# Down projection of a transformer layer as seven half-size products instead of eight

## The reference, cut to what matters

```python
def conv_ffn(h, w_up, conv_w, conv_b, w_down):
    z = h @ w_up                                  # 512 x 1024 times 1024 x 5632
    ...
    a, u = jnp.split(zc, 2, axis=-1)              # zc: a causal convolution of width 3 over z
    return (jax.nn.silu(a) * u) @ w_down          # 512 x 2816 times 2816 x 1024

x = x + conv_ffn(rms_norm(x, norm_ffn_g[l]), ...)
return rms_norm(x, final_norm_g)
```

## Time and profile before

| | us |
|---|---|
| median of 3 runs (965.14 to 965.41) | 965.34 |
| span of the profiled execution | 963.6 |
| around the span (median less span) | 1.7 |
| TensorE busy | 951.7 (99%) |
| VectorE busy | 563.3 (58%) |
| ScalarE busy | 390.9 (41%) |
| GpSimd busy | 34.6 (4%) |

### The profile page before, as it was taken

The page is one execution under the profiler, slowest core; times in us unless marked ns, Lnnn a source line. Parts: engine busy times, 40 slices in busy tenths (PEclk is TensorE's granted clock), DMA queues, the critical chain, the costliest instruction groups (busy, mean ns, idle before and its releaser), DMA issues.

```text
span 963.6 us, 12000 instructions
## 1 busy us (share of the span) xinstructions
PE 951.7 (99%) x4782; PEld 796.8 (83%) x4782; DVE 563.3 (58%) x646; ACT 390.9 (41%) x427; POOL 34.6 (4%) x27
## 2 busy tenths in 40 slices
PE   8999999999999999999999999999999999999997
PEld 6899889777888788888888878888888888888886
DVE  5877654554677564466545548776777677711123
ACT  6473223332664552333333446444434444311122
POOL 1000000200000000000021005000000000000000
PEclk9999999999999999999999999999999999999999
DMA  7414212122232523333223224343333432222212
GB/s 253 160 44 131 73 59 88 46 79 62 66 95 81 178 76 97 98 98 120 90 91 126 79 75 131 88 127 92 87 87 104 113 87 87 92 103 111 88 44 88
DMA packets 121570, 93.80 MB, mean 97 GB/s; under 512 B 3930, under 2 KB 115902, under 8 KB 121406
## 3 DMA queue, kind: packets, MB, share of 16 engines
q1 hardware_dynamic: 121534, 93.27, 31.4%
HBM read 91.16 MB, written 2.10 MB: 97 GB/s over the span
## 4 chain that ended last, share of the span: by engine, by line
PE 91%; DVE 4%; ACT 3%; issue 1%; DMA 0%; SPq 0%; DVEq 0%; ACTq 0%
PE ps L496 66%; PE ps L999 12%; PE ps L860 5%; DVE wL L1345 1%; PE ps L540 1%; PE ps L640 1%; PE ps L631 1%; PE ps L624 1%; ACT wH L1029 1%; PE ps L874 1%; PE ps L890 1%; ACT L1029 1%; PE ps L646 1%; DVE hgF L1345 0%; DVE hgG L1537 0%
## 5 line engine op out<-in xcount | busy, mean ns | idle before, releaser
L496 PE MATMUL ps<-hH,wH 128*128 128x512 f32 x784 | 308.5, 394 | 4.1 <-DVE wL L1345 3.8
L496 PE MATMUL ps<-hH,wL 128*128 128x512 f32 x784 | 305.3, 389 | 0.0
L496 PE MATMUL ps<-hL,wH 128*128 128x512 f32 x784 | 305.2, 389 | 0.0
L1345 DVE TENSOR_TENSOR wL<-raw,wH 128x2048 fp32r<-128x2048 f32 (+3 forms) x90 | 188.4, 2094 | 130.9 <-ACT wH L1029 130.7
L1029 ACT ACTIVATE wH<-raw 128x2048 fp32r<-128x2048 f32 (+3 forms) x90 | 157.7, 1752 | 227.5 <-PE ps L496 146.3
L496 PEld LDWEIGHTS ps<-hH,wH 128*128 128x128 f32 x784 | 147.2, 188 | 37.9 <-DVE wL L1345 5.6
L496 PEld LDWEIGHTS ps<-hH,wL 128*128 128x128 f32 x784 | 147.1, 188 | 31.0
L496 PEld LDWEIGHTS ps<-hL,wH 128*128 128x128 f32 x784 | 147.2, 188 | 30.0 <-issue 0.2
L999 PE MATMUL ps<-wH,actH 128*128 128x512 f32 x176 | 68.7, 390 | 0.0
L999 PE MATMUL ps<-wH,actL 128*128 128x512 f32 x176 | 68.5, 389 | 0.0
L999 PE MATMUL ps<-wL,actH 128*128 128x512 f32 x176 | 68.5, 389 | 0.0
(11 more groups left out here) (275 smaller groups left out, 1225.4 us busy)
## 6 DMA issues: line engine op xcount, KB each, us to landing
raw<-in_w_in SPq DMA_DIRECT2D x57, 512.0 KB, 4.1
raw<-in_w_up SPq DMA_DIRECT2D x44, 512.0 KB, 4.6
raw<-in_w_down SPq DMA_DIRECT2D x22, 512.0 KB, 3.9
raw<-in_w_branch SPq DMA_DIRECT2D x24, 256.0 KB, 4.3
raw<-in_w_out SPq DMA_DIRECT2D x8, 512.0 KB, 4.1
raw<-in_w_mkv SPq DMA_DIRECT2D x8, 512.0 KB, 4.4
xtok<-in_x SPq DMA_DIRECT2D x8, 256.0 KB, 4.4
xtok<-in_x SPq DMA_DIRECT2D x1, 2048.0 KB, 9.1
```

The lines of the kernel that those rows point to most:

```text
L496: last = pe.matmul(out_ap, a, b, start=start and k + m == 0, stop=stop and m == 2 and k == len(terms) - 1)
L1345: q.sig(dve.tensor_tensor(out_ap, a, b, op), sem)
```

## The change

The down projection is done by one level of Strassen's scheme (Winograd's form). Tokens, the 2816 channels and the 1024 output columns are each cut in two halves, and instead of eight products of halves there are seven, of sums of halves. The 1408 channels of a half make 11 pairs of 128-row blocks, and `NP` is 11.

The up projection takes its slots in another order, tile i of the first half and then tile i of the second, and `prod` goes into one array `pair` of seven half-token blocks of 256 for each pair, which VectorE completes with four additions (`act_sums`). `actH`, `actL`, ScalarE's copy and VectorE's subtraction of the activation go from the up loop. All 22 slots are still there, the last two written out after a loop of ten turns.

The down projection has 22 steps. In each of the first 11 ("upper") four products are done, 24 matmuls: ScalarE makes four upper parts (512, 1024, 512 and 1024 numbers wide), VectorE four lower parts of the same sizes and, in between, three sums of 512 from the raw weights of the next step (`weight_sums`). In each of the other 11 ("lower") three products are done, 18 matmuls: ScalarE copies 768, 1024 and 512, VectorE adds 512 and subtracts 768, 1024 and 512. Raw weights are loaded twice in part: 768 KB an upper step, 512 KB a lower one. Operands of a step are in two buffers by turns, and ScalarE's first copy into one waits for TensorE's end of the step two before (`d_done`). Between the upper and the lower steps VectorE combines the four finished products with additions of 1024 out of the banks, the residual's 32 transposes go into banks in groups of eight, and the lower steps add on top. The last two lower steps are done together, product by product and token tile by token tile, so that pieces finish one by one. ScalarE loads the table for the square roots in the fifth lower step. At the end VectorE adds the stored parts, ScalarE squares out of `otok`, GpSimd multiplies three pieces by the gain ahead of time, VectorE and ScalarE scale, and six DMAs store the output. The final gain's load goes behind the first two down loads in SyncE's order.

```diff
-        actH = at("actH", A, [P, KF, S], F32R)
-        actL = at("actL", A + 44 * KIB, [P, KF, S], F32R)
...
+        pair = at("pair", A, [P, NP, 7, HT])
...
-            def load_down(n, j):
-
-                v = raw[n.s][:, :].rearrange("p (k c) -> p k c", k=2)
-                load(n, *((v[:, k, :], wdn[:, 2 * j + k, :]) for k in range(2)))
+            def load_down(i):
+                n = Slot(N_DN + i)
+                if i < 2:
+                    sp.wait_ge(lo_ready, n.n(-1))
+                else:
+                    sp.wait_ge(d_lo, lows(i - 2, 1))
+                    sp.wait_ge(d_t, 2 * (i - 2) + 2)
+                rows = slice(P * i, P * i + P)
+                low = slice(FF // 2 + P * i, FF // 2 + P * i + P)
+                sp.dma_start(raw[n.s][:, 0:D], w_down[0, rows, :]).then_inc(raw_in[n.s], 16)
+                sp.dma_start(raw[n.s][:, D:D + S], w_down[0, low, S:D]).then_inc(raw_in[n.s], 16)
+            def load_lower(i):
+                g = NP + i
+                s = (N_DN + g) % 2
+                if i < 2:
+                    sp.wait_ge(d_lo, lows(g - 2, 1))
+                    sp.wait_ge(d_t, 2 * (g - 2) + 2)
+                else:
+                    sp.wait_ge(d_lo, lows(g - 2, 2))
+                    sp.wait_ge(d_t4, i - 1)
+                sp.dma_start(raw[s][:, 0:D], w_down[0, FF // 2 + P * i:FF // 2 + P * i + P, :]).then_inc(d_in[s], 16)
...
-            sp.wait_ge(slot_done, N_MO)
+            with sp.Fori(0, NP) as i:
+                for k in range(2):
+                    load_up(Slot(N_UP + k, i, 2), i + NP * k)
+            for i in range(2):
+                load_down(i)
+            sp.wait_ge(slot_done, N_DN)
             sp.dma_start(gainF[:, :], final_norm_g.partition_broadcast(P)).then_inc(g_row, 16)
-            with sp.Fori(0, KF // 2) as i:
...
+            lo_half, hi_half = slice(0, S), slice(S, D)
+            sp.wait_ge(o_fin, 1)
+            sp.dma_start(osrc[:, 2, :], otok[:, 2, :]).then_inc(out_done, 16)
+            sp.wait_ge(o_act, 1)
+            sp.wait_ge(o_fin, 2)
+            sp.dma_start(osrc[:, 3, :], otok[:, 3, :]).then_inc(out_done, 16)
+            sp.wait_ge(o_fin, 3)
+            sp.dma_start(osrc[:, 0, hi_half], otok[:, 0, hi_half]).then_inc(out_done, 16)
+            sp.wait_ge(o_act, 2)
+            sp.dma_start(osrc[:, 0, lo_half], otok[:, 0, lo_half]).then_inc(out_done, 16)
+            sp.wait_ge(o_fin, 4)
+            sp.dma_start(osrc[:, 1, hi_half], otok[:, 1, hi_half]).then_inc(out_done, 16)
+            sp.wait_ge(o_act, 3)
+            sp.dma_start(osrc[:, 1, lo_half], otok[:, 1, lo_half]).then_inc(out_done, 16)
+            sp.wait_ge(out_done, 16 * 6)
...
+            pool.wait_ge(g_row, 16)
+            pool.wait_ge(d_out, 5)
+            pool.wait_ge(d_lo, lows(NP, 0))
+            pool.tensor_tensor(g22[:, :], otok[:, 3, S:D], gainF[:, S:D], ALU.mult).then_inc(d_gain, 1)
+            for t in range(2):
+                pool.wait_ge(d_out, 6 + t)
+                pool.tensor_tensor(g11[:, t, :], otok[:, t, 0:S], gainF[:, 0:S], ALU.mult).then_inc(d_gain, 1)
...
+            def half_product(g, q, b, start, stop, tiles=(0, 1)):
+                s = (N_DN + g) % 2
+                for t in tiles:
+                    ah, al = (x[s][:, q, P * t:P * t + P] for x in (sH, sL))
+                    for m, (x, w) in enumerate(((ah, wH), (ah, wL), (al, wH))):
+                        last = pe.matmul(ps[:, b + t, :], x, w[s][:, S * q:S * q + S], start=start and m == 0,
+                                         stop=stop and m == 2, skip_group_check=True)
+                return last
...
+            for i in range(NP):
+                for q, b in enumerate((4, 6, 2, 0)):
+                    if q == 0:
+                        pe.wait_ge(d_lo, lows(i, 2))
+                    elif q < 3:
+                        pe.wait_ge(d_lo, lows(i, 2 + q))
+                    if i == 0 and q >= 2:
+                        pe.wait_ge(taken, N_DN - 3 + q)
+                    last = half_product(i, q, b, i == 0, i == NP - 1)
+                    if i == NP - 1:
+                        last.then_inc(d_sum, 1)
+                if i < NP - 1:
+                    last.then_inc(d_done, 1)
+            for i in range(NP - 2):
+                g = NP + i
+                for q, b in enumerate((4, 6, 0)):
+                    if i == 0:
+                        if q == 0:
+                            pe.wait_ge(d_m1, 1)
+                        else:
+                            pe.wait_ge(d_out, (1, 3)[q - 1])
+                        residual((2, 3) if q == 2 else (0, 1), range(4, 8) if q == 1 else range(4), b)
+                    pe.wait_ge(d_lo, lows(g, (2, 2, 3)[q]))
+                    last = half_product(g, q, b, False, False)
+                last.then_inc(d_done, 1)
+                if i == 0:
+                    pe.wait_ge(d_out, 4)
+                    residual((2, 3), range(4, 8), 2).then_inc(d_sum, 1)
+            for q, b in ((0, 4), (2, 0), (1, 6)):
+                for t in range(2):
+                    for g in (2 * NP - 2, 2 * NP - 1):
+                        pe.wait_ge(d_lo, lows(g, 3))
+                        last = half_product(g, q, b, False, g == 2 * NP - 1, (t,))
+                    last.then_inc(d_sum, 1)
...
-                hi(n + 2)
-                act.wait_ge(f_prod, n.n(1 - N_UP))
-                do(actH[:, bass.ds(n.n(-N_UP), 1), :], prod[:, :], ACT.Copy, f_hi)
...
+            def down_upper(i):
+                n = Slot(N_DN + i)
+                act.wait_ge(raw_in[n.s], n.loads())
+                if i < 2:
+                    act.wait_ge(slot_done, n.n(-1))
+                else:
+                    act.wait_ge(d_done, i - 1)
+                upper(i, wH[n.s][:, 0:S], raw[n.s][:, 0:S])
+                act.wait_ge(f_sum, 4 * i + 4)
+                upper(i, sH[n.s][:, :, :], pair[:, i, 0:4, :])
+                act.wait_ge(d_t, 2 * i + 2)
+                upper(i, wH[n.s][:, S:2 * S], t2_of(i))
+                upper(i, wH[n.s][:, 2 * S:4 * S], tsum[n.s][:, :, :].rearrange("p q c -> p (q c)"))
+            def lower_upper(i):
+                g = NP + i
+                s = (N_DN + g) % 2
+                if i == 1:
+                    act.wait_ge(d_sum, 4)
+                else:
+                    act.wait_ge(d_done, g - 1 if i == 0 else g - 2)
+                upper(g, sH[s][:, 0:3, :], pair[:, i, 4:7, :])
+                act.wait_ge(d_in[s], 16 * (i // 2 + 1))
+                upper(g, wH[s][:, 0:D], raw[s][:, 0:D])
+                act.wait_ge(d_t4, i + 1)
+                upper(g, wH[s][:, D:D + S], t2_of(i))
...
+            for i in range(NP):
+                lower_upper(i)
+                if i == 0:
+                    act.wait_ge(d_sum, 1)
+                    do(m1[:, :, :], ps[:, 4:6, :], ACT.Copy, d_m1)
+                if i == 4:
+                    act.wait_ge(d_out, 5)
+                    for t in (2, 3):
+                        square_of(t, 1, o_sum)
+                    do(ostat[:, 0, 5:6], eps[:, 0:1], ACT.Sqrt)
...
+            def act_sums(i):
+                j = bass.ds(i, 1)
+                dve.wait_ge(f_prod, i * 2 + 2)
+                tt(pair[:, j, 2, :], pair[:, j, 6, :], pair[:, j, 3, :], ALU.subtract, f_sum)
+                dve.wait_ge(f_sum, i * 4 + 1)
+                tt(pair[:, j, 1, :], pair[:, j, 0, :], pair[:, j, 2, :], ALU.add, f_sum)
+                tt(pair[:, j, 3, :], pair[:, j, 0, :], pair[:, j, 3, :], ALU.subtract, f_sum)
+                dve.wait_ge(f_sum, i * 4 + 2)
+                tt(pair[:, j, 5, :], pair[:, j, 4, :], pair[:, j, 1, :], ALU.subtract, f_sum)
...
+            def weight_sums(i):
+                n = Slot(N_DN + i)
+                dve.wait_ge(raw_in[n.s], n.loads())
+                if i >= 2:
+                    dve.wait_ge(d_lo, lows(i - 2, 4))
+                w, t = raw[n.s], tsum[n.s]
+                tt(t[:, 0, :], w[:, 0:S], w[:, S:D], ALU.add, d_t1)
+                tt(t[:, 1, :], w[:, S:D], w[:, D:D + S], ALU.add, d_t)
+                dve.wait_ge(d_t1, i + 1)
+                if i:
+                    dve.wait_ge(d_lo, lows(i - 1, 2))
+                tt(t2_of(i), t[:, 0, :], w[:, D:D + S], ALU.add, d_t)
+            def down_lower(i):
+                n = Slot(N_DN + i)
+                dve.wait_ge(d_hi, lows(i, 1))
+                rest(wL[n.s][:, 0:S], raw[n.s][:, 0:S], wH[n.s][:, 0:S])
+                dve.wait_ge(d_hi, lows(i, 2))
+                rest(sL[n.s][:, :, :], pair[:, i, 0:4, :], sH[n.s][:, :, :])
+                if i + 1 < NP:
+                    weight_sums(i + 1)
+                dve.wait_ge(d_hi, lows(i, 3))
+                rest(wL[n.s][:, S:2 * S], t2_of(i), wH[n.s][:, S:2 * S])
+                dve.wait_ge(d_hi, lows(i, 4))
+                rest(wL[n.s][:, 2 * S:4 * S], tsum[n.s][:, :, :].rearrange("p q c -> p (q c)"), wH[n.s][:, 2 * S:4 * S])
+            def lower_lower(i):
+                g = NP + i
```

(69 more changed lines are left out.)

211 lines of the change are left out of this document (106 added, 105 removed).

## The result

The change makes the kernel slower. The median of four runs after is 978.2 us (977.12 to 979.66), that of the kernel before beside them 965.38 us: a ratio of 1.0131, with a 95% interval from 1.0117 to 1.0146. The forecast was 963.9 with a range of 960.5 to 969.5, so the result lies outside it. The span of the profiled execution is 977.9 us, 14.3 more than before; it is the longest of the four, which is why this is more than the 12.8 between the medians.

The account below looks back on a forecast made before the run. TensorE was taken to bound the kernel up to the last matmul. Terms -15.0 + 0.2 + 6.8 + 0 + 0.8 + 3.4 + 2.3 = -1.5 gave 963.9 us, range 961.5 to 966.5, or 960.5 to 969.5 with most of two rivals.

Parts of the forecast that it names:

- the sentence on the up loop: Up loop: work removed and added lies beside 10.9 us of matmuls a slot and moves nothing until the last two slots.
- rival B: Down stage: TensorE's long stalls make its clock fall, 1.3 to 3 us lost, 965.2 to 967; chance 0.13.
- the two forecast waits of 3.6 and 3.4: TensorE stalls at down step 1 (3.6 us) and before the last products (3.4 us).
- The matmuls, 66 fewer: Down projection: 528 matmuls become 462, at 0.2268 us each, saving 15.0 us.
- The start: First down steps: TensorE waits for VectorE's chain through the last tiles and its lower parts; 6.8 us lost.
- The bank's wait: Down step 0: the fourth product waits for a bank until slot 76's second read ends; 0.6 us lost.
- step 2 (1.6): Down step 2: pair 10's additions stand ahead of its parts; 0.55 and 1.05 us lost.
- rival A: Upper steps: VectorE becomes the bound through gaps between instructions, 967.2 at 0.05 us each, 969.9 at 0.08; chance 0.20.
- The table load in the fifth lower step: Lower step 5: squares, table load and root make ScalarE's next copies 1.4 us late; 0.8 us lost.
- rival C: Lower step 5: ScalarE stands still another 1.28 us behind the table load, all lost, 965.2; chance 0.05.
- The last wait: Last two lower steps: TensorE waits for step 21's lower parts, whose buffers step 19 holds; 3.4 us lost.
- The tail: After the last matmul: additions, scalings and DMAs end 7.4 us behind its result instead of 5.1; +2.3 us.

Follow-up runs that it names:

- e1: The changed kernel with one single-column ScalarE silu ahead of the up projection's loop, so no table load is inside it; 967.59 us, ratio 1.0019.
- e3: e1 with 12 extra matmuls into an unused bank, where TensorE waits for the last step's lower parts; 965.75 us.
- e4: e1 with the last two lower steps run one after the other instead of interleaved; 963.80 us, ratio 0.9982.
- e6: e5 with the buffers behind the tile products moved by 448 bytes, the second sH and sL among them; 958.58 us, ratio 0.9927.
- e5: e4 with VectorE's sums, lower parts and pair 10's additions in another order at the start of the down stage; 960.77 us, ratio 0.9940.

## Why the prediction was wrong

**The step that failed** is the sentence on the up loop: what comes there "lies beside 10.9 us of matmuls a slot and moves nothing". It compared VectorE's and ScalarE's work with TensorE's, engine by engine. What had to be compared is the chain that goes back and forth between the two, 9.81 us of the 10.9. The room was in the earlier trace rows: VectorE waits 1.07 for TensorE before `zu`, so a turn of two slots has 2.14 to spare. The additions take 1.62 and fit. The table load takes another 1.28, and 2.90 - 2.14 = 0.76 a turn is what was measured. That the load comes was not thought of at all: the text of the change names a table load in the down stage only, but it takes away the two written-out slots, and with them the silu that stood ahead of the loop. Cost of the step: the term was put at 0 and measured 9.1 us, of which 8.1 go with the loads (e1) and 1.0 comes with the first turn; the late VectorE cost another 2.8 at the start of the down stage.

**The clock** was rival B, at 0.13, priced at 1.3 to 3 us for one fall. It happened, twice in the profiled execution; by e1 and e3 each fall cost 1.5 us there, the first of them out of a stretch 2.8 us longer than at full rate. The price was right, the chance too low: the one row I had, 3.2 us of standstill, is as long as the two forecast waits of 3.6 and 3.4, and I counted it against the rival that no row shows a fall between matmuls. But before TensorE never waits in the down stage, so that absence said nothing. Nor did the sum see that a fall at a place where VectorE sets the pace can cost nothing, as in e4. The Trainium skill (TensorE: Matmul & The Clock Gate, HAM oscillation) says that waits between bursts of matmuls are paid again at half clock; the rows above agree for the last wait in the kernel after and in e1, and for the first in the kernel after and in e4, but not for the first in e1 and e3.

**The down stage otherwise.** Forecast 119.4, measured 125.36, 5.9 more. Of these 4.3 are the two half-rate stretches, which took the place of 1.3 us of waits at the start. The rest by terms:

- The matmuls, 66 fewer: forecast and found. But their distance was not 0.2268 everywhere. The runs of matmuls between the waits take 1.8 us more than at that distance; the addresses moved in e6 take 1.6 of the same 1.8 away, and its down stage is 1.2 shorter. The term was mis-sized by using the distance of one operand layout for another.
- The start: forecast 6.8, found 7.35, each wait counted from the matmul before with the restart: 0.9 at 847.21, 2.0 at 851.97, 3.55 at 856.92, 0.9 at 859.34. The long one (forecast 3.6) and the one behind it (1.05) were right. The bank's wait (0.6) was 2.0 because the loop had left VectorE late, the one at 847.21 was not foreseen, and step 2 (1.6) had none: the half clock had given VectorE time. In e1, where neither the loop nor the clock disturbs it, the start is 5.8: 3.55, 1.0, 0.2 and 1.0, and no wait for the bank. So the total came near 6.8 in part by luck.
- Upper steps: none of the waits of rival A. From 865 to 905 us VectorE is busy 38.74 of 40.00, with instructions of 512 at 0.60 and of 1024 at 1.13 from start to start, as forecast, and TensorE never waits:

```profile
865.00:905.00 40.00, 40.00 (x174) 32.56 (x173) 38.74 (x52) 21.37 (x28) 0.00 (x0) 1.00 0.41 140
```

- The table load in the fifth lower step: forecast 0.8, found 0.26 (36 matmuls take 8.42 up to 940.67 instead of 8.16). The root holds ScalarE for 0.11 instead of 0.30, so it is free 5.5 us after the step began, not 5.7; the rest of the difference is that TensorE had more in hand than the 0.6 counted. The first instruction behind the load starts at once, so rival C's other 1.28 us did not come. The Trainium skill (ScalarE: Activation LUTs, What ACT_TABLE_LOAD costs) gives the load the same 1283 ns as the page of the profile, but the drain it adds is in none of these rows:

```profile
936.18 1.28 ACT L1109 ACT_TABLE_LOAD   x1
937.47 0.20 ACT L1109 ACTIVATE ostat<-eps 128x1 f32<-128x1 f32 x1
```

- The last wait: forecast 3.4, found 3.2 (957.84 to 961.28, less 0.23). The tail: forecast 7.4 behind the last result, 7.6 behind the end of the last matmul, found 7.55, the DMAs leaving at 970.0 to 974.6.

**Point by point against "what would show it":** 462 matmuls, yes, at 227 ns only in every second step; a wait of 3.6 six us behind the up loop, 3.3 there, but eight behind because of the two ahead of it; none from step 3 to 10, yes; 3.4 before the last, 3.2; VectorE over 90%, yes (97%); the clock at 1.00, no; 7.4 at the end, yes. With e1, where the table loads alone are taken out of the loop, the time is 967.59, inside the range and 3.7 above the forecast. From `ones` on it is 362.0 against 359.2, 2.8 more: 1.0 in the up projection, with the wait of 0.78 in its first turn, and 1.9 in the down stage, where the clock (1.5) and the matmuls' distance (1.8) are partly paid by a start and a table load that cost less than forecast (1.0 and 0.5). The other 0.9 lie ahead of `ones`, where the clock fell near 13 us in e1's profile and not in that of the kernel before.

## What to carry to other kernels

When work is added beside a bound engine, compare it not with that engine's time but with what the dependent chain through the helping engines leaves of it; one wait for the bound engine per turn in the trace gives that room. When instructions ahead of a hardware loop go away, ask what state the loop's body now finds at its entry: here a table, loaded twice in each of ten turns. The two long waits of TensorE were priced right as waits (6.8 us) and cost 3.0 more through the clock, so a scheme that trades matmuls for waits should first get its sums ahead (e5) rather than its matmul count down. What a fall of the clock costs is not the length of the slow stretch: where another engine sets the pace right behind it, the slow matmuls only fill waits (e4: nothing lost), and where nothing else holds them up, all of it is lost (e1 against e3: 1.55).

## What was not expected of the hardware

- Behind a wait of 3.3 us at the same place the clock fell in two profiles (after, e4) and not in two others (e1, e3); behind one of 2.0 to 2.4 us near the start of the span it fell in four of eight. A fall makes 7 to 14 distances 0.427 us and costs 0 to 1.5 us by what follows. Medians of two kernels can differ by the 1.0 us of the fall near the start, so distances from a mark behind it compare better.
- Operand addresses seem to change a matmul's distance. Up to e5 the second `sH` and `sL` lie 64 bytes past a multiple of 512, and the steps that use them run at 0.233 us a matmul of 128x512; with 448 bytes more (e6) at 0.227, as the others.
- VectorE is slower beside GpSimd's product. In the kernel after, `sL` of 768 takes 1.40 us beside it; in the next step, with GpSimd idle, the same instruction takes 0.96 (at 933.15). GpSimd's product takes 1.62 there and 1.29 near the end. All six changed kernels show the pair (1.40 to 1.49 against 0.96):

```profile
928.03 1.62 POOL L547 TENSOR_TENSOR g<-otok,gainF 128x512 f32<-128x512 f32 x1 [324.85 <-DVE otok L1475]
```

```profile
929.06 1.40 DVE L1475 TENSOR_TENSOR sL<-pair,sH 128x768 fp32r<-128x768 f32 x1 [0.57 <-ACT sH L1109]
```

It cost nothing here, since VectorE was ahead. It was the 0 to 0.5 left open in the prediction.
